# Rows of the last two experts slotted in on chip, and the first row tiles loaded before the last scatters

## The reference

```python
h2 = rmsnorm(x, norm2_g) * (1 + sc2) + sh2
x = x + g2 * hier_moe(h2, ...)       # 32 experts, each token goes to 2 of them
y = rmsnorm(x, final_g)              # row by row

# in hier_moe: gates is (tokens, 32), zero but for the token's two experts
a = silu(einsum('td,edf->tef', t, w_gate)) * einsum('td,edf->tef', t, w_up) * gates[:, :, None]
y = einsum('tef,efd->td', a, w_down)
```

## Time and profile before

| | |
|---|---|
| median of 3 runs | 887.52 us (887.51 to 888.49) |
| the profiled execution, its own time | 894.03 us |
| its span from first to last instruction | 891.9 us |
| PE busy | 855.0 us (96%), of 4471 matmuls |
| DVE busy | 672.1 us (75%) |
| ACT busy | 465.1 us (52%) |
| POOL busy | 236.0 us (26%) |
| TensorE's mean granted clock | 0.990 of full speed |
| chain that ended last, by engine | PE 76%, DMA 8%, DVE 6%, issue 4%, ACT 3%, POOL 2% |

### The profile page before, as it was taken

How to read it: one execution, slowest core, us unless ns; L and a number is a source line. 1 busy time by engine, 2 the same in 40 slices (tenths; PEclk the granted TensorE clock), 3 DMA queues, 4 the chain that set the end, 5 groups by cost and what they waited for, 6 DMA issues and landing times.

```text
span 891.9 us, 12151 instructions
## 1 busy us (share of the span) xinstructions
PE 855.0 (96%) x4471; PEld 684.0 (77%) x4471; DVE 672.1 (75%) x1019; ACT 465.1 (52%) x695; POOL 236.0 (26%) x212
## 2 busy tenths in 40 slices
PE   5999999999998999999999989999999999999985
PEld 4889999999986555578888857777777777777652
DVE  5657786968756777456888667988888788887758
ACT  6551111112215777544444617778777777677543
POOL 1000000000025777533012242332332223321134
PEclk9999999999999999999999999999999999999999
DMA  9731534524211112152121478999999999998487
GB/s 366 322 123 48 212 121 190 189 71 165 69 29 31 48 49 103 10 212 87 56 76 67 192 300 322 377 384 376 376 375 371 373 386 373 368 368 334 162 342 303
DMA packets 42148, 194.54 MB, mean 218 GB/s; under 512 B 12167, under 2 KB 13127, under 8 KB 25319
## 3 DMA queue, kind: packets, MB, share of 16 engines
q1 hardware_dynamic: 32376, 174.24, 52.1%
q0 software_dynamic: 9712, 19.52, 5.8%
HBM read 182.00 MB, written 26.41 MB: 234 GB/s over the span
## 4 chain that ended last, share of the span: by engine, by line
PE 76%; DMA 8%; DVE 6%; issue 4%; ACT 3%; POOL 2%; SPq 0%; DVEq 0%; ACTq 0%; POOLq 0%
PE PS L968 9%; PE PS L970 8%; PE PS L972 8%; PE PS L2562 5%; PE PS L2563 5%; PE PS L2564 5%; PE PS L2611 4%; DMA w_gu<-in_w_gu 4%; PE PS L1775 3%; PE PS L1777 3%; PE PS L1776 3%; PE PS L1082 3%; PE PS L1113 3%; PE PS L1133 3%; PE PS L2551 2%
## 5 line engine op out<-in xcount | busy, mean ns | idle before, releaser
L968 PE MATMUL PS<-h_hi,w_hi 128*128 128x384 f32 (+1 forms) x432 | 147.5, 342 | 1.9 <-DVE h_lo L678 1.3
L970 PE MATMUL PS<-h_lo,w_hi 128*128 128x384 f32 (+1 forms) x432 | 146.3, 339 | 0.0
L972 PE MATMUL PS<-h_hi,w_lo 128*128 128x384 f32 (+1 forms) x432 | 145.7, 337 | 0.0
L2337 DVE TENSOR_TENSOR gu_lo<-w_gu,gu_hi 128x2048 fp32r<-128x2048 f32 x53 | 121.0, 2283 | 2.3 <-ACT gu_hi L2203 2.3
L2203 ACT ACTIVATE gu_hi<-w_gu 128x2048 fp32r<-128x2048 f32 x53 | 101.7, 1918 | 23.2 <-DMA w_gu<-in_w_gu 23.2
L2562 PE MATMUL PS<-gu_hi,xT_hi 128*128 128x512 f32 x256 | 104.6, 409 | 1.2 <-DVE xT_lo L2395 1.2
L2563 PE MATMUL PS<-gu_lo,xT_hi 128*128 128x512 f32 x256 | 101.2, 395 | 0.0
L2564 PE MATMUL PS<-gu_hi,xT_lo 128*128 128x512 f32 x256 | 101.2, 395 | 0.0
L2146 POOL DMA_INDIRECT y_rows<-yrows,tab x31 | 37.3, 1203 | 207.4 <-DVE yrows L2368 207.4
L968 PEld LDWEIGHTS PS<-h_hi,w_hi 128*128 128x128 f32 x432 | 81.3, 188 | 8.3 <-issue 7.0
L970 PEld LDWEIGHTS PS<-h_lo,w_hi 128*128 128x128 f32 x432 | 81.7, 189 | 0.0
(11 more groups left out here) (300 smaller groups left out, 1785.3 us busy)
## 6 DMA issues: line engine op xcount, KB each, us to landing
w_gu<-in_w_gu SPq DMA_DIRECT2D x55, 1024.0 KB, 14.3
w_d<-in_w_down SPq DMA_DIRECT2D x32, 1024.0 KB, 14.4
wm<-in_w_mod SPq DMA_DIRECT2D x16, 1024.0 KB, 5.3
w_raw<-in_w_in SPq DMA_DIRECT2D x18, 512.0 KB, 6.1
gu_raw<-in_w_gu SPq DMA_DIRECT2D x9, 1024.0 KB, 15.0
yt<-y_rows SPq DMA_DIRECT2D x9, 1024.0 KB, 15.0
xt<-in_x_all SPq DMA_DIRECT2D x9, 512.0 KB, 3.8
y_all<-yt SPq DMA_DIRECT2D x9, 512.0 KB, 3.5
```

Source lines behind the costliest of these rows:

```text
L968: pe.matmul(o, w_hi[b][:, k, :], h_hi[:, k, tok], start=k == 0, stop=False)
L970: pe.matmul(o, w_hi[b][:, k, :], h_lo[:, k, tok], start=False, stop=False)
L972: last = pe.matmul(o, w_lo[b][:, k, :], h_hi[:, k, tok], start=False, stop=k == KD - 1)
L2337: dve.tensor_tensor(low_half(i), raw_half(i), raw(high_half(i)), ALU.subtract).then_inc(s_lo, 1)
```

## The change

- ORDER becomes [8, 7, 6, 5, 4, 3, 2, 1, 0], and a table ROOM says which slot of `yt` a tile is loaded into.
- The rows of expert 30 that belong to tiles 8 and 7 are no longer scattered (the scatter's bound is lowered, so that higher rows are dropped). A second scatter of zeros ahead of the experts clears them. ACT and DVE split the expert's result (`other_hi`, `other_lo`), DVE builds two matrices for it, and PE adds it for those two tiles (`from_other`).
- Expert 31 is slotted in on chip for the first five tiles (SLOTTED) only. For the other four its rows are scattered: POOL issues that scatter after its second pair sum.
- SP issues the first load after the scatter of expert 29, the second when the last gate and up product is done, the third to fifth after the scatter of expert 30, the last four after the scatter of expert 31.
- POOL adds the row pairs of the first eight tiles. DVE adds the residual in SBUF, to the pair sum, for tiles 1 to 4 of the order (`residual`), and PE then adds that to PSUM in `from_rows`. Tile 5's residual is added by PE (`from_x`), its scaling is done by ACT (Copy with a scale) and POOL (times `fg`). Tiles 6 and 7 never go through PSUM (`shared`, and `finish` from SBUF). The last tile is done half in PSUM, half in SBUF, and stored in two halves.

```diff
-        ORDER = [1, 2, 3, 4, 8, 5, 6, 0, 7]
+        ORDER = [8, 7, 6, 5, 4, 3, 2, 1, 0]
+        ROOM = [7, 1, 2, 3, 4, 5, 6, 0, 8]
+        SLOTTED, FROM_PE, SHARED = 5, 5, (6, 7)
+        PRE_ADDED = (1, 2, 3, 4)
+        FIRST = 2
-        DVE_SUMS = ORDER[1:2]
-        POOL_SUMS = ORDER[2:9]
+        POOL_SUMS = ORDER[:-1]
...
@@ sync @@
-                    for b in range(2):
-                        sp.wait_ge(s_out[b], 16 * (NE // 2 - b))
-                    for t in ORDER:
+                    for i, t in enumerate(ORDER):
+                        if i == 0:
+                            for b in range(2):
+                                sp.wait_ge(s_out[b], 16 * (NE // 2 - 1))
+                        elif i == FIRST:
+                            sp.wait_ge(s_out[0], 16 * (NE // 2))
+                        elif i == SLOTTED:
+                            sp.wait_ge(s_out[1], 16 * (NE // 2))
...
                     for i, t in enumerate(ORDER):
-                        sp.wait_ge(s_fin, fin_base + i + 1)
...
+                        if i == FROM_PE:
+                            sp.wait_ge(s_psum, psum_base + NT)
+                        else:
+                            sp.wait_ge(s_fin, fin_base + i + (1 if i < FROM_PE else 0))
@@ gpsimd @@
+                    for n in range(HELD - 1, HELD + 1):
+                        pool.indirect_dma_start(
...
+                            bounds_check=TOPK * P * tiles_stored(n) - 1,
...
-                    for t in POOL_SUMS:
+                    for i, t in enumerate(POOL_SUMS):
+                        if i == 2:
+                            scatter(HELD)
                         pool.wait_ge(s_yt[t], yt_base + 16)
...
+                    t = ORDER[FROM_PE]
+                    pool.wait_ge(s_scaled, scaled_base + 1)
+                    pool.tensor_tensor(yt[:, ROOM[t], 0, :], yt[:, ROOM[t], 0, :], fg, ALU.mult
+                                       ).then_inc(s_psum, 1)
@@ scalar @@
+                            act.wait_ge(s_gu, 2 * n + 1)
+                            act.wait_ge(s_y, n)
+                            act.activation(other_hi, yrows[:, (n - 1) % 2, :], ACT.Copy
+                                           ).then_inc(s_other, 1)
...
+                    for i, t in enumerate(ORDER[:-1]):
+                        square(i, t)
+                        if i == FROM_PE + 1:
+                            s = ORDER[FROM_PE]
+                            act.wait_ge(s_fr, fr_base + FROM_PE + 1)
+                            act.activation(halves(yt[:, ROOM[s], 0, :]), sum_banks(FROM_PE), ACT.Copy,
+                                           scale=fss[:, s, 2:3]).then_inc(s_scaled, 1)
@@ vector @@
+                    def residual(i, t):
+                        x = yt[:, ROOM[t], 0, :].rearrange("p (k n) -> p k n", n=P)
+                        dve.wait_ge(s_psum, psum_base + i + 1)
+                        dve.tensor_tensor(x, x, tile(cat, t), ALU.add).then_inc(s_resid, 1)
...
+                    residual(1, ORDER[1])
+                    combine_first(ORDER[0])
+                    residual(2, ORDER[2])
+                    residual(3, ORDER[3])
+                    rooted(0)
+                    residual(4, ORDER[4])
+                    rooted(1)
+                    rooted(2)
+                    shared(6, ORDER[6])
+                    shared(7, ORDER[7])
+                    rooted(3)
+                    last_combine(ORDER[-1])
+                    rooted(4)
+                    inverse_root(FROM_PE, ORDER[FROM_PE])
+                    rooted(6)
+                    rooted(7)
...
+                    last_finish(ORDER[-1])
@@ tensor @@
+                    from_other(0, True)
+                    from_held(0, ORDER[0], False)
+                    from_rows(0, ORDER[0])
+                    from_other(1, True)
+                    from_held(1, ORDER[1], False)
+                    pe.wait_ge(s_y, NE)
+                    from_held(2, ORDER[2])
+                    from_held(3, ORDER[3])
+                    from_rows(1, ORDER[1])
+                    from_rows(2, ORDER[2])
+                    pe.wait_ge(s_fin, fin_base + 1)
+                    from_held(4, ORDER[4])
+                    from_rows(3, ORDER[3])
+                    from_rows(4, ORDER[4])
+                    pe.wait_ge(s_fin, fin_base + 2)
+                    from_x(FROM_PE, ORDER[FROM_PE], range(2))
+                    from_rows(FROM_PE, ORDER[FROM_PE])
```

More of the change, by code:

```diff
@@ L2012, in build @@
             held_hi, held_lo = gu_hi1[:, 0, 0:D], gu_hi1[:, 1, 0:D]
+            other_hi, other_lo = gu_lo6[:, 0:D], gu_lo6[:, D:2 * D]
             def raw_half(i):
@@ L2695, in _, with from_x, from_rows, from_held @@
                     overflow(pe, one_round)
[L2697 to L2704 removed]
+                    def from_x(i, t, halves_of):
+                        for half in halves_of:
+                            last = pe.matmul(
+                                sum_banks(i)[:, half, :].rearrange("p (k n) -> p k n", n=P),
+                                ident[:], tile(cat, t)[:, HALF_CHUNKS[half], :], start=True,
+                                stop=False)
+                        return last
+                    def from_rows(i, t):
+                        if i in PRE_ADDED:
+                            pe.wait_ge(s_resid, PRE_ADDED.index(i) + 1)
+                        else:
+                            pe.wait_ge(s_psum, psum_base + i + 1)
                         for half in range(2):
[L2706 to L2716 removed]
+                            last = pe.matmul(sum_banks(i)[:, half, :], ident[:],
+                                             yt[:, ROOM[t], 0, half * 512:half * 512 + 512],
+                                             start=False, stop=True)
+                        last.then_inc(s_sum, 1)
+                    def from_held(i, t, first=True):
+                        pe.wait_ge(s_heldhot, heldhot_base + i + 1)
                         for half in range(2):
@@ new lines, in from_held, with from_other @@
+                        return last
+                    def from_other(i, first):
+                        pe.wait_ge(s_otherhot, otherhot_base + FIRST + 1)
+                        for half in range(2):
+                            cols = slice(half * 512, half * 512 + 512)
+                            o = sum_banks(i)[:, half, :]
+                            pe.matmul(o, other_rows(i), other_hi[:, cols], start=first, stop=False)
+                            last = pe.matmul(o, other_rows(i), other_lo[:, cols], start=False,
+                                             stop=False)
@@ new lines, in _ @@
+                    from_rows(3, ORDER[3])
[3 more added lines that the diff above has]
+                    from_rows(FROM_PE, ORDER[FROM_PE])
+                    pe.wait_ge(s_fin, fin_base + 3)
+                    from_x(NT - 1, ORDER[-1], range(1))
+                    pe.wait_ge(s_yt[ORDER[-1]], yt_base + 16)
+                    for k in range(TOPK):
+                        last = pe.matmul(sum_banks(NT - 1)[:, 0, :], ident[:],
+                                         yt[:, ROOM[ORDER[-1]], k, 0:512], start=False,
+                                         stop=k == TOPK - 1)
```

186 lines of the change are left out of this document (100 added, 86 removed).

## The result

| | before | changed |
|---|---|---|
| median of 22 runs each | 889.08 us (885.59 to 894.92) | 892.83 us (889.06 to 896.39) |
| ratio, 95% interval | | 1.0037 [1.0022, 1.0052] |
| profiled execution, its own time and span | 894.03, 891.9 us | 892.02, 890.2 us |
| last silu of expert 31 to the end of the span | 42.1 us | 45.9 us |
| TensorE's mean granted clock | 0.990 | 0.992 |

A forecast was written before the change was run, and what follows sets the result against it. Bound before: a tail pipeline started by expert 30's scatter landing. Last landing 3.8 us earlier, but blocked POOL sums, DVE's order and queued stores end the span at 893.9, 2.0 later: 887.52 + 2.0 = 889.5 us, range 884.5 to 892.3.

The forecast's parts named there:

- the likeliest case: Tail: POOL's sums and DVE's operations with two SBUF inputs block each other; span 2.0 us longer, 889.5 us, chance 0.45.
- The loads: Tail loads on SP: first issued at 845.1, second landing at 854.5; only one of nine early by 5 us.
- The cover: During expert 31: ACT's `other_hi` copy (about 1.0 us), DVE's two matrices and subtraction are hidden by PE's product.
- The blocking: Tail: each DVE operation with two SBUF inputs costs POOL about 1.1 us and waits up to 2.37 itself.
- the signs: Tail, if right: POOL's pair sums above 3 us, `residual` and `shared` on DVE at 2 us and more.
- Rival 1: Tail: POOL and DVE don't hinder each other; no change, 887.5 us, chance 0.28.
- The end: Behind `shared` 7 (879.3): DVE's steps, ACT's late copy, POOL's multiplication and five queued stores end the span at 893.9.
- Rival 2: Tail: the 13.8 us behind the last landing stay, so 3.8 us are gained: 883.7 us, chance 0.13.
- five matrices in place of nine save DVE 0.8 us where it waits for PE anyway: Last expert's matrices on DVE: fewer of them, at 0.2 us each, save 0.8 us during a wait for PE.
- who holds SBUF: Tail: listed `residual`, `shared`, `last_combine` and `finish` 6 and 7 as DVE's SBUF additions, each costing POOL about 1.1 us.
- Rival 3: Tail: PE idles near 869, TensorE's clock halves, end 1 to 3 us after the forecast: 890.5 to 892.5, chance 0.14.
- The scatter's landing: Expert 31's scatter on POOL: starts at 857.6, takes 5.2 us, lands at 862.8; the last four loads wait for it.

The follow-up runs named there:

- e4: The changed kernel with each of POOL's eight pair sums replaced by two memsets that read nothing from SBUF: ratio 1.0021, 890.78 us.
- e7: The changed kernel with tile 5 finished by DVE from PSUM, without ACT's scaled copy and POOL's multiplication: ratio 1.0016, 890.81 us.
- e1: The changed kernel, but POOL waits for the last expert's five matrices before its first pair sum: ratio 1.006, 892.99 us.
- e5: The changed kernel with 17 useless matmuls while PE waits for the last expert's split rows: ratio 1.0041, 892.0 us.
- e2: The changed kernel with POOL waiting for the five matrices before its sums and issuing the last scatter after its first sum: ratio 1.0084, 897.25 us.
- m1: The kernel before plus new order, early loads and expert 30's slotted rows; nine POOL sums after the matrices, DVE adding in PSUM: ratio 0.9989, 887.5 us.
- m3: The kernel before with early loads, PSUM additions, POOL waiting for matrices and split, and PE doing expert 30's second-tile part first: ratio 0.9964, 886.76 us.
- e8: The kernel before, but DVE adds the fourth tile's residual in SBUF ahead of PE's matmul, not in PSUM: ratio 1.0049, 894.3 us.
- e6: The changed kernel with ACT's scaled copy of tile 5 behind tile 7's square, and tile 5's store after tiles 6 and 7: ratio 1.0042, 892.82 us.

## Why the prediction was right and wrong

The sign of the likeliest case was right and its size too small. Of the distance from 889.5 to 892.83, the tail makes 1.8: +2.0 was forecast and +3.8 measured. The rest, 1.6, is the base: 887.52 was the median of three runs, 22 gave 889.08, and the profile of before (894.03) had already shown that runs spread that far. On that base the same sum gives 891.1.

Right, step by step, in us after the silu:
- The loads. The first was issued at 839.70, 4.6 before the silu (4.7 forecast), and the second at the silu, landing 4.8 and 4.9 later. Only one load of nine is early by 5 us, as worked out.
- The cover. Expert 30's copy, matrices and subtraction lie under the last gate and up product, as costed; the last silu waited 1.69 us for PE, not for ACT.
- The blocking, as a mechanism: three of the four `residual` took 1.7 to 3.4 instead of 1.22, and the last three sums 9.03 instead of 7.4. It was less even than the signs had it: the other five sums stayed at 2.4 to 2.5 each, and the two `shared`, forecast at 2 us and more, took 1.2. Rival 1, no hindrance, is out by these rows; e4, without the sums' reads, has a tail 2.6 shorter.
- The end. From `shared` 7 to the end of the span 14.6 were forecast and 14.8 measured, with the scaled copy late and `finish` 7 stretched. e7 confirms that this path, not PE, set it.
- Rival 2, faster because the 13.8 us behind the last landing stay, is out as well: the last landing came only 1.5 us earlier than before (26.8 after the silu against 28.3; 24.5 forecast), and 19.1 us followed it.

Wrong: the way from the silu to the end of `shared` 7, 29.5 forecast and 31.2 measured. The step that failed is "five matrices in place of nine save DVE 0.8 us where it waits for PE anyway". It was costed alone, ahead of the section on who holds SBUF, although these operations have two inputs in SBUF as `residual` has, and the forecast put POOL's sum 0 at 850.9, beside them. Four of the five took 5.26 us where they take 0.89 without a sum (e1, e4), and all five 5.55 where the nine of before took 1.98. So the term was 3.6 us of cost and not 0.8 of gain. The split of the expert's rows began 6.4 us after the silu before, and 9.1 after it now. PE stood 3.84 us for it, the clock fell, and the first combine came at 15.5. Rival 3 was thus real as an event, some 10 us ahead of the place it was put at, but at most 0.7 of it reached the end (e5) where I gave 1 to 3.

From there the path was another than forecast. The forecast let `shared` 6 wait for sum 7, at the end of POOL's chain. In the run DVE came to it 0.5 us after sum 7 had ended, straight from its own queue, which had no gap since the first combine. Taking the matrices' stretch away gives back at most 1.0 of the 1.7 us: in e1 `shared` 7 ended 30.2 after the silu, since the split and `residual` 1 then met the same sums. So how much of the 1.7 belongs to these matrices is not shown. What is shown is that the list of hindered operations left out those ahead of the first tile.

The scatter's landing was mis-sized too, 14.4 after the silu and not 13.0. I added a landing time to an issue; the later issue (9.8 after the silu, 7.8 forecast) is not why, since e2 issued it at 6.7 and it landed at 14.8. In the changed kernel this had no price that shows, as DVE was later still; with the sums' reads gone (e4) it stands in the chain that ended last.

The sizes don't add up to 3.8 and needn't: e4 takes away the blocking by the sums for 2.6, e7 POOL's multiplication alone for about 2, e5 the clock for 0.7 or less, and each uncovers the next. Against before, m1 to m3 show that the early loads don't cost the time; what the change adds besides does. That of these it is chiefly DVE's steps in SBUF, standing ahead of PE's, is argued from e4 and e8; no run takes them alone out of the changed kernel.

What stays open: how long a blocked DVE instruction waits. It was let in after one sum in e8, after two in e1 and after three in e2, behind back-to-back sums of one shape in each. I found no rule in the timelines for it: in e1 the addition's record starts even before that of the first sum it waited for (855.28, when the split had not quite ended, and 855.64). It also wasn't tried whether the scatter would land earlier with its own rows issued ahead of load 4.

## What to carry to other kernels

Before giving GpSimd and VectorE work in SBUF side by side, list every VectorE instruction with two SBUF inputs in that stretch, the small ones too, and ask of each who waits for it: four 0.2 us matrices in front of the longest chain were stretched by 4.4 us here, the worst of the 1.22 us additions by 2.1. Freeing one of them hands the hindrance to the next (e1). What helped was to let GpSimd wait until the steps that TensorE needs were through (m3). An addition that stands behind TensorE (in PSUM) costs its own time; the same addition ahead of TensorE puts both engines' queues, and TensorE's clock, behind it. Where a sum is made on the spread of a few runs, put the spread of the base into the range.

## What the runs showed of the hardware

- A blocked VectorE instruction may wait for more than the one it met: 1.57, 6.13 and 7.94 us for one of 1.22 beside gapless sums of 2.36. The Trainium skill ("SBUF — State Buffer", section "Summary: rules for kernel authors") says that the second to issue blocks until the first finishes; the first of the three fits, the other two outlast it by one and two sums.
- An operation of 128x128 with two SBUF inputs is held as one of 128x1024 is: four took 5.26 us instead of 0.89 (5.24 in e6 and in e7).
- An indirect scatter issued by GpSimd while loads of 1 MB are in flight landed 2.2 to 2.5 us after the last of them in four kernels, from issues 3.1 us apart.
- One and the same wait of PE doesn't cost one and the same time at the lower clock. In the changed kernel PE stood 3.84 us, and the granted clock was 0.50 for about 7 us (853 to 860), though PE worked again from 854.22. In e7 PE stood 3.81 us, until 855.34, and the clock means were 0.68, 0.50 and 0.97 in the three stretches of 2 us from 854 on, which makes about 3.4 us at 0.50.
